# Differential attention, last head: the low parts of the turned probabilities are taken one slot later, behind the next slot's maxima

## The reference

```python
def block(qb):
    sc = jnp.einsum('bqhcd,bkhcd->bhcqk', qb, k).astype(f32) * scale
    p = jax.nn.softmax(sc, axis=-1)
    a = (p[:, :, 0] - lam * p[:, :, 1]).astype(v.dtype)
    return jnp.einsum('bhqk,bkhe->bqhe', a, v)
o = from_blocks(lax.map(block, to_blocks(q)))
o = (rmsnorm(o) * (1.0 - lam_init)).astype(h.dtype)
```

## Time and profile before

| | us |
|---|---|
| median of 3 runs | 2812.7 |
| lowest, highest | 2812.21, 2812.94 |
| the profiled execution | 2812.84 |
| its span in the profile | 2811.1 |

### The profile page before, as it was taken

One profiled execution on the slowest core, in us unless ns is written; L12 is line 12 of the kernel. 1 busy time (PEld: TensorE's weight loads), 2 busy tenths in 40 slices (PEclk: granted clock), 3 DMA queues, 4 the chain that ended last, 5 costly groups with the idle time before them and its releaser, 6 DMA issues. The chain is left out here.

```text
span 2811.1 us, 40206 instructions
## 1 busy us (share of the span) xinstructions
PE 2725.6 (97%) x13716; PEld 2266.0 (81%) x13716; DVE 1778.2 (63%) x2479; ACT 1354.7 (48%) x2096; POOL 1408.5 (50%) x1081
## 2 busy tenths in 40 slices
PE   8999999999899999999999999998898999999998
PEld 7788888888778888888777777776787888888886
DVE  6677777772755555555688888887428555455554
ACT  5577777772444444311356666665324444443112
POOL 1355555553687777644333222221246877775444
PEclk9999999999999999999999999999999999999999
DMA  3000000004022222522030000000321222225221
GB/s 140 26 10 8 7 7 10 15 2 179 30 90 90 72 85 90 202 100 109 15 115 31 31 31 31 31 24 23 157 98 46 90 90 76 81 96 203 90 89 60
DMA packets 54391, 195.35 MB, mean 69 GB/s; under 512 B 6544, under 2 KB 9872, under 8 KB 53776
## 3 DMA queue, kind: packets, MB, share of 16 engines
q1 hardware_dynamic: 54288, 193.95, 19.0%
HBM read 148.84 MB, written 45.09 MB: 69 GB/s over the span
## 5 line engine op out<-in xcount | busy, mean ns | idle before, releaser
L1331 PE MATMUL ffn_ps<-ffn_b,weights_hi 128*128 128x512 f32 x704 | 277.7, 394 | 17.9 <-issue 10.9
L1332 PE MATMUL ffn_ps<-ffn_b,weights_hi 128*128 128x512 f32 x704 | 276.3, 392 | 0.0
L1333 PE MATMUL ffn_ps<-ffn_b,weights_lo 128*128 128x512 f32 x704 | 276.2, 392 | 0.0
L1207 POOL TENSOR_TENSOR ffn_y_lo<-ffn_y_raw,ffn_y_hi 128x1024 fp32r<-128x1024 f32 x44 | 107.0, 2453 | 236.1 <-ACT ffn_y_hi L1128 236.1
L799 POOL TENSOR_TENSOR up_local_lo<-up_sums,up_local_hi 128x512 fp32r<-128x512 f32 x126 | 170.2, 1353 | 106.9 <-ACT up_local_hi L794 106.9
L409 POOL TENSOR_TENSOR weights_lo<-weights_raw,weights_hi 128x1024 fp32r<-128x1024 f32 (+2 forms) x64 | 124.6, 1951 | 185.0 <-ACT weights_hi L404 185.0
L2527 ACT ACTIVATE dif_p<-dif_s,dif_neg_max 128x1024 f32<-128x1024 f32 x128 | 142.3, 1114 | 135.1 <-DVE dif_neg_max L2735 116.5
L1331 PE MATMUL ffn_ps<-ffn_b,up_local_hi 128*128 128x512 f32 x504 | 196.2, 389 | 1.0 <-issue 1.0
L1333 PE MATMUL ffn_ps<-ffn_b,up_local_lo 128*128 128x512 f32 x504 | 196.1, 389 | 0.0
L1332 PE MATMUL ffn_ps<-ffn_b,up_local_hi 128*128 128x512 f32 x504 | 196.1, 389 | 0.0
L1128 ACT ACTIVATE ffn_y_hi<-ffn_y_raw 128x1024 fp32r<-128x1024 f32 x44 | 44.2, 1051 | 315.0 <-PE ffn_ps L1333 315.0
(11 more groups left out here) (412 smaller groups left out, 8200.9 us busy)
## 6 DMA issues: line engine op xcount, KB each, us to landing
weights_raw<-in_up SPq DMA_DIRECT2D x44, 512.0 KB, 3.8
up_raw<-in_up SPq DMA_DIRECT2D x44, 512.0 KB, 4.2
ffn_products<-ffn_conv SPq DMA_DIRECT2D x44, 512.0 KB, 2.6
ffn_y_raw<-ffn_products SPq DMA_DIRECT2D x44, 512.0 KB, 4.1
ffn_down_raw<-in_down SPq DMA_DIRECT2D x24, 512.0 KB, 6.8
weights_raw<-in_diff_qkv SPq DMA_DIRECT2D x23, 512.0 KB, 3.5
weights_raw<-in_down SPq DMA_DIRECT2D x20, 512.0 KB, 6.6
x_spill<-x_in SPq DMA_DIRECT2D x16, 512.0 KB, 4.0
```

The costliest lines, as they stand in the source:

```text
L1331: pe.matmul(out, hi, x_hi, start=start, stop=False, skip_group_check=True)
L1332: pe.matmul(out, hi, x_lo, start=False, stop=False, skip_group_check=True)
L1333: return pe.matmul(out, lo, x_hi, start=False, stop=stop, skip_group_check=True)
```

## The change

In the last head, in the slots with scores from t = 1 on, VectorE no longer takes the low parts of turn n-1 behind the mix of slot n. From t = 2 on it takes those of turn n-2 directly behind the maxima of slot n. The first slot behind the scores (n = 64) takes two pairs: those of turn 62 and those of turn 63. All other heads, and slot 0 of the last head, keep their order. No other engine's program is changed.

```diff
+            def low_probs(n, t, behind):
+
+                m, tm = n - behind, (t - behind) % HT
+                for half in range(2):
+                    dve.wait_ge(pt_hi_done, 2 * m + (half + 1))
+                    part = (slice(None), slice(4 * half, 4 * half + 4), slice((tm % 2) * P, (tm % 2 + 1) * P))
+                    dve.tensor_tensor(pt_lo[(tm // 2) % 2][part], turn_ps[half][:].rearrange("p (k m) -> p k m", m=P),
+                                      pt_hi[(tm // 2) % 2][part].bitcast(F32), ALU.subtract).then_inc(pt_lo_done, 1)
+
             def slot(h, parity, t, n, first, scores, more):
+                in_last = scores and not more
                 if t == LAG_V and not first and not more:
                     take_sums(h, 1 - parity)
                 turn = not (first and t == 0) and (scores or t == 0)
-                tm = (t - 1) % HT
                 if scores:
                     for m in range(2):
                         col = 2 * (t % 2) + m
                         dve.wait_ge(scores_ready, 2 * n + (m + 1))
                         dve.tensor_reduce(neg_max[:, col:col + 1], s_ps[m][:], AX_X, ALU.max,
                                           negate=True).then_inc(max_ready, 1)
+                    if in_last and t >= 2:
+                        low_probs(n, t, 2)
...
-                if turn:
-                    for half in range(2):
-                        dve.wait_ge(pt_hi_done, 2 * n + (half - 1))
-                        part = (slice(None), slice(4 * half, 4 * half + 4), slice((tm % 2) * P, (tm % 2 + 1) * P))
-                        dve.tensor_tensor(pt_lo[(tm // 2) % 2][part], turn_ps[half][:].rearrange("p (k m) -> p k m", m=P),
-                                          pt_hi[(tm // 2) % 2][part].bitcast(F32), ALU.subtract).then_inc(pt_lo_done, 1)
+                if turn and not (in_last and t >= 1):
+                    if not scores:
+                        low_probs(n, t, 2)
+                    low_probs(n, t, 1)
```

## The result

| | kernel before | changed kernel |
|---|---|---|
| median, lowest to highest, first comparison (18 runs each) | 2814.84 us, 2810.07 to 2817.68 | 2818.9 us, 2815.93 to 2821.65 |
| ratio | | 1.0017, 95% interval 1.0011 to 1.0023 |
| second comparison (26 and 10 runs) | 2812.09 us | 2819.34 us |
| ratio | | 1.0026, 95% interval 1.0017 to 1.0036 |
| span of the profiled execution | 2811.1 us | 2817.3 us |

The changed kernel is slower, by 4 us in the first comparison and 7 us in the second, of some 2813 us. The measured time lies inside the forecast range, 1.7 us above the forecast of 2817.2 us; but the forecast took that for no measurable difference, and the comparison can tell it.

What follows compares the result with a forecast made beforehand. TensorE, busy 97% of the span, was taken as the bound, with the last-ending wait deciding each slot of the changed stretch. 3.67 + 1.5 = 5.2, less 0.7, gives +4.5 us on 2812.84: forecast 2817.2 us, range 2814.5 to 2819.6.

Steps and rivals of the forecast that it cites:

- Slot 2, +3.67 us: Slot 2's turning waits for the late low part, starting at 1945.32 instead of 1941.65; V1 projection and next scores follow.
- Clock under the projection, 1.5 us: After some 3.8 us idle in slot 2, TensorE's clock falls to 1.2 GHz under the V1 projection, costing 1.5 us (0 to 1.7).
- D: Forecast delay at the scores of slot 3: 3.67 us of wait plus 1.5 us of clock, 5.2 us.
- What comes back, 0.7 us: Slot 7: turn 62's low part waits for its high part, not the mix, so the last turning regains 0.7 us.
- The tail, 0 us: Last turning and everything behind it (value products, square, sums, next stage) only move along, with no added time.
- rival (b): Waits of slots 4, 6 and 7 bring one more low stretch onto full work: +6.2 us, 2819.0 us; 17%.
- The size, +4.5 us: Whole kernel: 5.2 us delay less 0.7 us back gives +4.5 us, bounded by +2.5 and +5.4 us.
- What a measurement can tell, 0.2% or 5.6 us: Times from 2807.1 to 2818.3 us count as no change; faster 0.01, same 0.79, slower 0.20.
- GpSimd, 0 to 0.6 us: GpSimd's splits of the next weights could hold up VectorE's ratio in slot 7 by 0 to 0.6 us; taken as 0.
- (a): Clock does not fall in slot 2's new idle, or falls inside it: only the wait costs, +3.0 us, 2815.8 us; 17%.
- (c): The edit frees the path in all slots and TensorE's wait costs nothing: about -2.5 us, 2810.3 us; 5%.
- (d): The edit does not do what it says, for example the pair runs in the same place: 2812.8 us; 3%.

Runs made afterwards that it cites:

- Turn 56 alone: Changed kernel with only turn 56's low parts moved behind the maxima of slot 2, all others left as before; ratio to before 1.0018 [1.0009, 1.0027].
- without turn 56: Changed kernel with turn 56's low parts left in slot 1 and those of turns 57 to 62 moved; ratio to before 1.0001 [0.9992, 1.0010].
- the filled run: Changed kernel plus 12 added products of 128x512 ahead of slot 2's turning, their result overwritten; ratio to before 1.0009 [1.0000, 1.0018].
- projection first: Changed kernel with TensorE doing slot 2's V1 projection ahead of the turning; ratio to before 0.9998 [0.9988, 1.0007].
- kernel before with filling: Kernel before plus unused products: 10 and 7 behind the turnings of slots 4 and 6, 6 ahead of the last turning; ratio to before 0.9981 [0.9972, 0.9990].

## Why the prediction was right in its size and wrong in taking it for no difference

- **Slot 2, +3.67 us: right.** The idle time was 3.82 us and ended with the low part; the turning came 3.55 us later, counted from the maxima of slot 0 (18.04 against 14.49), and 3.66 us later from the scores of slot 1 (11.20 against 7.54). Turn 56 alone reproduces the loss, without turn 56 it is gone, and it goes too when the projection is put ahead of the wait.
- **Clock under the projection, 1.5 us: right, with some luck.** 1.3 us by the filled run. The forecast let the low clock last 3.4 us and bounded its price by 1.7 us; in two other profiles with the same wait it lasted 6.8 us and cost 2.5 to 2.6 us. At the scores of slot 3 the delay was 25.95 - 21.05 = 4.9 us, D was 5.2.
- **What comes back, 0.7 us: the sum about right, its way wrong.** The delay was 4.9 us at the scores of slot 4, 5.3 of slot 5 (the turning ahead of them ran at the lower clock, 1.94 instead of 1.03 us), 4.25 of slot 6, 5.1 of slot 7 and 4.76 at the last turning, for which I had 4.5. I had turn 62's low part freed from the mix by maxima of slot 7 that start earlier; those waited for scores at the lower clock, and the low part at 1990.06 still stood directly behind the mix.
- **The tail, 0 us: wrong.** I let everything behind the last turning move along unchanged. It became 1.5 us longer by a low clock, and of the sum's terms this is the one that was mis-sized: stage and tail are 6.3 us longer, beyond the upper bound of the sum, +5.4 us. This is what rival (b) describes, one more low stretch on full work, and its price is right: it gave 4.5 + 1.7 = +6.2 us. But its reason does not fit: it went by idle times of 2.7 us or more, and the one ahead of the last turning was 1.90 us, next to the 1.81 us of before at which the clock had stayed up. It was given 17%.
- **The size, +4.5 us.** The whole times differ by 4.1 and 7.3 us in the two comparisons, so they do not say whether 4.5 or 6.3 us is nearer; up to the next phase's projection the profiles give 4.3 to 6.5 us. That the forecast time came so close to the measured one is partly luck.
- **What a measurement can tell, 0.2% or 5.6 us: wrong, and this is the step that failed.** From it I gave 79% to "no difference". With 18 runs of each the interval was 0.06% to either side, some 1.7 us, and the measured 0.17% stands clear of no change. The mechanism spoke for "slower" with hardly a case against it (8% for no loss or a gain); what went wrong is the comparison of 4.5 us with 5.6 us, as if all below were the same. Even with the sum exactly right it would have given "no difference".
- **GpSimd, 0 to 0.6 us, taken as 0:** right for the changed kernel (0.05 us), but a real term of its neighbours, 0.9 to 1.0 us, and so above the 0.6 us that I kept for the range.
- **Rivals (a), (c) and (d):** (a) falls with the two windows of the clock; (c) with the idle time of 3.82 us; (d) with VectorE's timeline.

## What to carry to other kernels

When a step is put off on one engine because it has idle time there, look up who waits for it and what is queued behind that waiter: here the pairs of turns 57 to 61 could be put off at no cost (that of turn 62 stayed where it was, behind the last mix), and the pair of turn 56 could not, because a projection that nothing in that slot depended on stood behind the wait. Either leave that one alone or put the independent work ahead of the wait. And count an idle time of TensorE twice, once as itself and once as the low clock that may follow it. Before calling a forecast difference too small to measure, ask how many runs there will be and how far they spread.

## What the runs showed of the hardware that I had not expected

- The low clock has no single length. In the stage of the kernel before it lasted 3.4 us each time, and 6.8 us right behind it in the next phase; it lasted 6.8 us in slot 2 in two runs and 13.7 us, from slot 5 on, in one, with TensorE busy in most of it. (Windows of 0.25 us give these lengths; the 6.9 and 13.8 us above come from rounded means.) After one and the same idle time of 3.8 us in slot 2 it cost 1.3 us in two profiles and 2.5 to 2.6 us in two; after idle times of 2.4 us in slot 0 it did not fall in every profile, and after one of 2.84 us ahead of the last turning (projection first) it did not fall at all.
- It also falls where TensorE has hardly idled. In slot 5 of the kernel before it went low for 3.4 us in the middle of a values product, with TensorE at work without a break and only 0.38 us of idle time and sixteen products of 128x1 ahead of that; in the kernel before with filling, where slot 4's idle time was filled, it stayed up there too. The window of the kernel before:

```profile
1969.00:1973.00 4.00, 4.00 (x22) 3.84 (x21) 2.39 (x4) 2.61 (x6) 0.00 (x0) 0.57 0.02 4
```

- Products whose result is thrown away can pay for themselves: 23 of them (some 5.3 us of TensorE's time at 0.23 us each) in idle times of slots 4, 6 and the tail of the kernel before took S' from 53.04 to 50.80 us, and the whole to 0.9981 [0.9972, 0.9990].
- A VectorE instruction on 128x1 lasted 1.1 to 1.2 us instead of 0.22 where it met a GpSimd instruction, and ended with it; this hold-up limits how early VectorE's chain can come in slot 7.
